# State-space part of a hybrid decoder step: scaled C and masked B built ahead of a merge, first decay table ahead of the third merge, sample state updates over 64 rows

## The reference

```
for each chunk:                        # two prompt chunks of 128 tokens; the sample tokens
    acum   = cumsum(dt * a)            # per head
    decay  = exp(acum[t] - acum[s])    # for s <= t, else 0
    xdt    = x * dt
    y_diag = ((C @ B^T) * decay) @ xdt
    y_off  = (C @ h) * exp(acum)       # h: the state that the chunk starts from
    tail   = exp(acum[last] - acum)
    h      = h * exp(acum[last]) + (xdt * tail)^T @ B
    y      = y_diag + y_off
```

## Time and profile before

| | before |
|---|---|
| median of three runs | 2127.86 us |
| lowest and highest run | 2123.18, 2131.23 us |
| the profiled execution, its own time | 2122.7 us |
| its span, first to last instruction | 2121.0 us |
| PE / DVE / ACT busy | 96% / 20% / 15% of the span |
| mean granted TensorE clock | 0.983 of full speed |

### The profile page before, as it was taken

How to read it: one execution, slowest core, us unless ns; L and a number is a source line. 1 busy time by engine, 2 the same in 40 slices (tenths; PEclk the granted TensorE clock), 3 DMA queues, 4 the chain that set the end, 5 groups by cost and what they waited for, 6 DMA issues and landing times.

```text
span 2121.0 us, 40435 instructions
## 1 busy us (share of the span) xinstructions
PE 2032.1 (96%) x17072; PEld 1203.7 (57%) x17072; DVE 426.5 (20%) x1129; ACT 324.0 (15%) x850; POOL 107.7 (5%) x199
## 2 busy tenths in 40 slices
PE   8998998999999999899999799999999999999996
PEld 6876676777777778667777433343434243434333
DVE  2234564210000132437431300000000000000001
ACT  2243221110000123522211100010101000101010
POOL 2110130000000000120000000000000000000000
PEclk9999999999999999999999999999999999999998
DMA  8753652533333334453233699999999999999996
GB/s 305 283 202 115 207 207 94 220 119 132 129 136 139 117 118 144 156 199 142 102 120 119 235 400 383 416 383 416 388 414 391 381 385 408 390 407 392 406 401 257
DMA packets 97803, 549.28 MB, mean 259 GB/s; under 512 B 12736, under 2 KB 29152, under 8 KB 38880
## 3 DMA queue, kind: packets, MB, share of 16 engines
q1 hardware_dynamic: 84144, 492.82, 60.0%
q0 software_dynamic: 11472, 46.86, 6.2%
q10 hardware_dynamic: 2016, 7.08, 1.0%
HBM read 532.90 MB, written 22.13 MB: 262 GB/s over the span
## 4 chain that ended last, share of the span: by engine, by line
PE 51%; issue 44%; DVE 2%; ACT 1%; DMA 1%; POOL 1%; POOLq 0%; DVEq 0%; SPq 0%; ACTq 0%
PE bank L469 40%; PE bank L610 3%; PE bank L640 1%; PE bank L855 1%; PE bank L665 1%; ACT phase_region L1211 1%; PE bank L749 1%; PE bank L727 1%; PE bank L793 0%; DVE phase_region L1600 0%; PE bank L488 0%; PE bank L653 0%; PE bank L536 0%; PE bank L579 0%; POOL xn L1188 0%
## 5 line engine op out<-in xcount | busy, mean ns | idle before, releaser
L990 PE MATMUL bank<-wring,phase_region 128*32 128x512 f32 (+2 forms) x9728 | 873.4, 521 | 11.6 <-ACT phase_region L1211 8.5
L469 PE MATMUL bank<-xn,wring 128*128 128x288 f32 x2496 | 639.8, 415 | 5.7 <-DVE phase_region L1600 3.6
L990 PEld LDWEIGHTS bank<-wring,phase_region 128*32 128x32 f32 x9728 | 310.5, 110 | 569.2 <-issue 529.5
L469 PEld LDWEIGHTS bank<-xn,wring 128*128 128x128 f32 x2496 | 478.2, 194 | 146.2 <-issue 10.6
L1211 ACT ACTIVATE phase_region<-bank 128x384 f32<-128x384 f32 (+14 forms) x244 | 87.8, 440 | 427.5 <-PE bank L957 206.0
L469 PE MATMUL bank<-phase_region,wring 128*128 128x288 f32 x608 | 148.2, 407 | 3.1 <-DVE mark L1527 2.4
L469 PEld LDWEIGHTS bank<-phase_region,wring 128*128 128x128 f32 x608 | 115.3, 190 | 36.0 <-DVE mark L1527 3.4
L2066 DVE TENSOR_TENSOR tmp<-phase_region,bank 128x512 f32<-128x512 f32 x32 | 22.0, 688 | 544.0 <-PE bank L990 544.0
L1481 ACT ACTIVATE phase_region<-bank 128x512 f32<-128x512 f32 (+1 forms) x48 | 25.2, 543 | 537.2 <-PE bank L990 537.2
L2079 DVE COPY phase_region<-bank 32x256 f32<-32x256 f32 x32 | 13.5, 420 | 297.6 <-PE bank L990 297.3
L610 PE MATMUL bank<-pages,wring 128*64 128x128 f32 (+1 forms) x1024 | 58.9, 276 | 0.0
(11 more groups left out here) (332 smaller groups left out, 1154.6 us busy)
## 6 DMA issues: line engine op xcount, KB each, us to landing
wring<-in_wstream SPq DMA_DIRECT2D x449, 1024.0 KB, 7.4
pages<-in_cmp_pages POOLq DMA_DIRECT2D x64, 128.0 KB, 4.0
pages<-in_cmp_pages SPq DMA_DIRECT2D x64, 128.0 KB, 4.3
pages<-in_slc_pages SPq DMA_DIRECT2D x64, 128.0 KB, 4.5
pages<-in_slc_pages POOLq DMA_DIRECT2D x64, 128.0 KB, 4.5
out_win_keep<-in_win_rows POOLq DMA_DIRECT2D x2, 4064.0 KB, 28.1
y_rows<-phase_region ACTq DMA_DIRECT2D x18, 384.0 KB, 5.0
pages<-in_win_kT POOLq DMA_DIRECT2D x4, 1024.0 KB, 5.3
```

The lines of the kernel that those rows point to most:

```text
L469: mm = nc.tensor.matmul(ps[:, 0:width], wb, rhs(k), start=(k == 0), stop=(k == n - 1))
L990: mm = nc.tensor.matmul(ps[QT * q:QT * q + QT, 0:n], lhsT, w, start=start, stop=stop)
```

## The change

```diff
@@ TensorE, y of chunk c
                     if c > 0:
                         pe.wait_ge(S["cp_ready"], 2 * l + c)
+                    if c == 2:
+                        pe.wait_ge(S["hs_in"], 16 * (l + 1))
@@ TensorE, sample state updates
-                                                          bm[0:n, 2 * b2 + i, g * HD:(g + 1) * HD],
-                                                          xtl[0:n, g * 256:(g + 1) * 256], start=True, stop=True)
+                                                          bm[0:HD, 2 * b2 + i, g * HD:(g + 1) * HD],
+                                                          xtl[0:HD, g * 256:(g + 1) * 256], start=True, stop=True)
@@ VectorE
                 dve.wait_ge(S["oC_ready"], l + 1)
+
+                def decay_start(c):
+
+                    n = TILES[c][1]
+                    up = C("upto0") if c < 2 else C("upto2", TS)
+                    V.tensor_tensor(decay[0:n, 0:NH * n].rearrange("p (h t) -> p h t", h=NH), bc(up, 1, NH),
+                                    bc(dta[0:n, c, :], 2, n), ALU.mult).then_inc(S["dD_ready"], 1)
+
+                decay_start(0)
                 merge(2)
@@
-                    V.tensor_tensor(d3, bc(up, 1, NH), bc(dta[0:n, c, :], 2, n), ALU.mult).then_inc(S["dD_ready"], 1)
                     if c > 0:
+                        decay_start(c)
                         merge(2 * c + 2)
@@
                     signal("dec_ready")
-                    merge(2 * c + 3)
                     dve.wait_ge(S["eb_ready"], cc + 1)
-                    if c == 2:
-                        dve.wait_ge(S["hs_in"], 16 * (l + 1))
                     if c > 0:
...
                     if c == 2:
                         dve.wait_ge(S["btok_ready"], cc + 1)
-                        V.tensor_tensor(bm[0:n, :, :], bc(btok[0:n, :], 1, NB), bc(C("in_batch", TS), 2, P), ALU.mult)\
+                        V.tensor_tensor(bm[0:HD, :, :], bc(btok[0:HD, :], 1, NB), bc(C("in_batch", HD), 2, P), ALU.mult)\
                             .then_inc(S["bm_ready"], 1)
+                    merge(2 * c + 3)
+                    if c == 2:
+                        dve.wait_ge(S["hs_in"], 16 * (l + 1))
                     dve.wait_ge(S["xbcc_ready"], l + 1)
```

More of the change, by code:

```diff
@@ L1832, in _ @@
                     d3 = decay[0:n, 0:w].rearrange("p (h t) -> p h t", h=NH)
-                    up = C("upto0") if c < 2 else C("upto2", TS)
                     mk = C("decay_mask0") if c < 2 else C("decay_mask2", TS)
-                    V.tensor_tensor(d3, bc(up, 1, NH), bc(dta[0:n, c, :], 2, n), ALU.mult).then_inc(S["dD_ready"], 1)
                     if c > 0:
+                        decay_start(c)
                         merge(2 * c + 2)
```

## The result

| | before | change |
|---|---|---|
| median | 2127.41 us (5 runs, 2119.27 to 2131.23) | 2107.71 us (5 runs, 2101.64 to 2109.32) |
| ratio | 1 | 0.9898 [0.9873, 0.9923] |
| the profiled execution, its own time | 2122.7 us | 2107.71 us |
| its span | 2121.0 us | 2106.0 us |
| mean granted TensorE clock in it | 0.983 | 0.982 |

The change is faster by 19.7 us between the medians, and by 15.0 us between the two profiled executions. The forecast was 17.3 us and 2110.6.

A forecast was written before the change was run, and what follows sets the result against it. PE was taken to bound the kernel, busy 2032.1 of 2121.0 us. Closed holes (12.2 us) plus full clock in layer 1's state updates (5.1) gave 17.3 us: 2127.9 - 17.3 = 2110.6 us, range 2102 to 2120.

The forecast's parts named there:

- The three holes, 12.16 us: PE idle ahead of L788 (1.75 us) and ahead of y in chunks 1 (2.57) and 2 (1.76); all close, both layers.
- The new waits: DVE waits for ACT's `btok_ready`, PE for the sample states; both forecast to be met before they are needed.
- The fourth hole: I take it as staying: PE idle 1.01 us ahead of the state updates (L855), layer 0 only; forecast to stay, its cause unnamed.
- 64 rows in the state updates, 5.1 us in layer 1: State updates (L855): full clock back in layer 1, worth 5.1 us, and nothing in layer 0.
- the clock keeps 1.00 in chunk 1, with 64 and 128 rows: Chunk 1's y and state update, right behind a 2.57 us hole, keep full clock; cited for the clock gain.
- the hole of 1.01 us: PE's idle time ahead of L855 in layer 0; its remaining was cited for no clock gain there.
- The sum of 12.2 us: Total gain if the clock follows only how busy PE is: the closed holes count, 64 rows give 0.
- The clock falls and rises as before: Rival: holes close, the clock around the state updates is unchanged; 12.2 us gained, 2115.7 us; chance 0.25.
- Full clock in both layers: Rival: holes close and the clock stays 1.00 through both layers' updates, 11.4 us more; 2104.3 us; chance 0.14.
- No new wait: Rival: instructions arrive too slowly at chunk 2's small matmuls, 1.76 us back per layer; 8.7 us gained, 2119.2; chance 0.09.
- Two blocks of 64 rows: Slower rival: L855's blocks take turns and double its time, 14.1 us more against 12.2 saved; 2129.8 us; chance 0.04.

The follow-up runs named there:

- e3: Kernel before with only the first decay table moved ahead of merge 2, 32 rows; 2130.44 us, one run.
- e4: Kernel before with only scaled C and masked B moved ahead of the merge, 32 rows; 2118.08 us, one run.
- e2: Kernel before with 64 rows in the state updates and nothing moved; median 2127.19 us (12 runs), ratio 0.999.
- e1: The change with its state updates back on 32 rows, all three moves kept; median 2107.25 us (6 runs), ratio 0.9905 to the kernel before.
- f2: Three moves with 32 rows, run again beside the change on one chip; median 2112.01 us (6 runs), ratio 0.9932 to the kernel before.
- e5: The change with chunk 2's sample state updates put ahead of y, 64 rows; median 2098.53 us (6 runs), ratio 0.987 to the kernel before.
- e6: The change with the state updates ahead of y and on 32 rows; median 2101.73 us (6 runs), ratio 0.9883 to the kernel before.
- f1: The change run once more with no edit; median 2106.35 us (5 runs), ratio 0.991 to the kernel before.
- e8: The change without the 64 small state-term matmuls of chunk 2's y (result incomplete); 2089.18 and 2093.24 us, ratio 0.9836 to the kernel before.
- e7: The change with chunk 2's two halves of y split by a projection of merge 7; median 2100.74 us (5 runs), ratio 0.9874 to the kernel before.
- f4: The change with the halves of chunk 2's y split by a projection, run again; median 2099.97 us (5 runs), ratio 0.9885 to the kernel before.

## Why the number was right and one of its reasons wrong

**The three holes, 12.16 us: right.** All six closed, each by the move that the prediction gave it: e3 closes those at L788 and no other, e4 those ahead of y. The new waits (`btok_ready` on DVE, `hs_in` on PE) hold nothing up. The holes are worth a little more than their idle time. From the start of the projection ahead to the first matmul behind the hole, these rows of PE before give 331.46 - 324.86 = 6.60 us:

```profile
324.86 4.04 PE L469 MATMUL bank<-o_sc,wring 128*128 128x288 f32 x16
331.46 0.66 PE L822 MATMUL bank<-phase_region 128*64 128x128 f32 x8 [2.57 <-issue]
```

The change takes 328.09 - 324.12 = 3.97 there, 2.63 less. In the same way the hole in chunk 0 gives 5.79 - 3.88 = 1.91 and that in chunk 2 5.81 - 3.97 = 1.84. Twice their sum is 12.8 us. At full clock the change has 2082.3 - 2067.7 = 14.6 us less, with 0.9 either way; the other 1.8 us are not explained.

**"The fourth hole: I take it as staying": wrong, at little cost.** It is absent from the change and from all profiles with the moves, but also from e2 and e3, where the hole of 1.76 us still stands ahead of the small matmuls. That doesn't settle whether the change removed it: in layer 0 of e2 and e3 the clock falls within the small matmuls, and the updates start 3.98 us after y does, where before they started 3.86 us after it, hole included. A wait of that length would not show there. What causes the hole stays open.

**"64 rows in the state updates, 5.1 us in layer 1": this is the step that failed.** The prediction read "the clock keeps 1.00 in chunk 1, with 64 and 128 rows" as a property of rows, and the hole of 1.01 us as what keeps the clock low in layer 0. Neither holds. Without any hole, 64-row updates ran at 0.50 in both layers of the change (7.09 us in layer 1, where 3.5 were forecast), so of the 5.1 us nothing came in this way; with 32 rows instead (e1, f2) the time is the same within 3.4 us; and 64 rows alone (e2) give 0.999 [0.997, 1.0011]. What made the updates run at full clock is the order: directly behind the projection and ahead of the small matmuls they take 3.67 us, with 64 rows (e5) and with 32 (e6). That rows never matter is not shown: in layer 0 of e6 the clock fell right behind the 32-row updates.

**What stood in its place.** The cost of the low clock did fall, by 42.5 - 37.0 = 5.5 us (with 2.3 either way), but by way of the holes; that this is near the 5.1 us of the forecast is luck. Chunks 0 and 1 have eight holes in the two profiles where all stand (before 0 falls behind 4, e2 4 behind 4), two in e3 (2 falls) and two in e4 (1 fall): 7 falls in 12. With the hole closed there were none, in 4 places each of the change, e1, f1 and f2 and in 2 each of e3 and e4. A fall of 3.4 us costs 1.7 us of work at full clock, so four places at 7 in 12 are 4.0 us. Behind the small matmuls, or from within them on (e2, e3), the low stretch averaged 12.5 us where the hole of chunk 2 stood (before, e2, e3: four of 13.7, two of 10.2) and 9.9 us in the change, e1, e4, f1 and f2 (nine of 10.2, one of 6.8): half of 2.6 us, twice, is another 2.6. Together 6.6 us, by counts of a few profiles, against 5.5 by the mean clock of 49 runs. That the moves bring this back, and not the rows, shows in all four kernels taken together: with the moves (the change, e1, f2: 22 runs) the low clock costs 38.2 us, without them (before, e2: 51 runs) 42.4, so 4.2 less with 2.4 either way. The moves with 32 rows by themselves (39.1, so 3.3 less with 3.6 either way) don't show it alone. Most of the low clock lies outside this stretch: in the profile of the change its cost is 2106.0 x (1 - 0.982) = 37.9 us, or 76 us at 0.50, and the two low stretches here are 20.4 us of these. So the counts above are an account of one stretch and not of the whole. Why a hole is followed by a fall in some executions and not in others was not tried.

**The profiled execution.** It was in the faster third of the kernel before, at clock 0.983 where 39 runs average 0.980, and had no fall behind a hole in chunk 0 or 1. Its low clock cost 2121.0 x (1 - 0.983) = 36.1 us, against 42.5 on the mean. That is the main reason why the gain between profiles is 15.0 us and between the medians 19.7. Reading the "keeps 1.00 right behind an idle hole" from it was reading one case of several.

**The rule of the Trainium skill.** The Trainium skill, "TensorE: Matmul & The Clock Gate", Part 1, "What's actually happening", says that how busy PE has recently been sets its clock, and names no rows. In the change's order the runs agree that rows made no difference (e1, e2). In layer 0 of e5 and e6 the rule does not tell the two apart: PE is busy for 3.51 of 3.51 us in both, and the clock falls behind the 32 rows alone. The sum of 12.2 us that the prediction drew from it was too small, since the closed holes also gave clock back. And PE counted as busy throughout the small matmuls (2.69 of 2.69 us), and the clock fell behind them all the same: here the busy time of the profile did not foretell the fall.

**The rivals.** "The clock falls and rises as before" was right that 64 rows did not keep the clock up here, and wrong that the holes leave the clock alone. "Full clock in both layers" gave 2104.3, near the measured time by chance: the updates were slow in both. No new wait appeared. Two blocks of 64 rows do run side by side: 32 records of 256 columns take 3.67 us, with 32 rows and with 64, and at 0.50 7.09 us.

## What to carry to other kernels

Where a run of very small matmuls is followed by a drop in the granted clock, look at what stands right behind it: put full-size work between its halves, or move the work that would run slowly ahead of it, here 6 to 8 us for a reordering with no work saved. A short idle hole on the bounding engine can cost more than its length, because the clock may fall behind it. Split every gain into span times mean granted clock and the rest, over many runs: the product moved by 1.3 us from run to run where the times moved by 5.4 (standard deviation, kernel before), and one profiled execution can be the lucky one.

## What the runs showed that I had not expected

The clock fell behind holes of 1.75 and 2.57 us, in some executions only, and then for 3.4 us with PE busy on L793 and L469 (e2). The 128 four-token matmuls of chunk 2 in the two layers cost 15.4 us by the span, though they last 4.4 us: 11.9 us of it is what ran at 0.50 behind them and elsewhere (e8). And with 2.21 us of full-size matmuls behind each half of the small ones the clock read 1.00 through the whole stretch, in both layers of both profiles (e7, f4). Once, in layer 0 of e6, the clock fell right behind updates of 32 rows, with hardly any small matmul done, where the same updates with 64 rows kept 1.00 (e5).
